# Conditioning vectors in two parts: mixing shift and scale first in row slabs on four column groups, the rest in the natural projection

## What is computed

```python
def adaln(c, w_ada, b_ada):
    return jnp.split(jax.nn.silu(c) @ w_ada + b_ada, 6, axis=-1)   # c: one row each for prompt and sample

def modulate(x, g, shift, scale):
    return rmsnorm(x, g) * (1.0 + scale[:, None, :]) + shift[:, None, :]

p_sh1, p_sc1, p_gt1, p_sh2, p_sc2, p_gt2 = adaln(c_prompt, w_ada[l], b_ada[l])
s_sh1, s_sc1, s_gt1, s_sh2, s_sc2, s_gt2 = adaln(c_sample, w_ada[l], b_ada[l])
...
qa, ka, va, qb, kb, vb, qi, ki, wi = jnp.split(h @ w_in, offs, axis=-1)      # h = modulate(x, g_mix_pre, sh1, sc1)
...
bias = rel_table[:, clip(rel, -128, 128) + 128]                              # by relative position, both attentions
...
yp = yp + p_gt1[:, None, :] * rmsnorm(mp, g_mix_post[l])
```

## Time and profile before

| | us |
|---|---|
| median of three runs | 1901.26 |
| the three runs | 1900.42, 1901.26, 1905.14 |
| the profiled execution | 1904.8 |
| its span, first instruction to last | 1902.9 |

### The profile page before, as it was taken

One profiled execution on the slowest core, in us unless ns is written; L12 is line 12 of the kernel. 1 busy time (PEld: TensorE's weight loads), 2 busy tenths in 40 slices (PEclk: granted clock), 3 DMA queues, 4 the chain that ended last, 5 costly groups with the idle time before them and its releaser, 6 DMA issues. The chain is left out here.

```text
span 1902.9 us, 23599 instructions
## 1 busy us (share of the span) xinstructions
PE 1767.8 (93%) x9129; PEld 1384.4 (73%) x9129; DVE 818.4 (43%) x1600; ACT 657.1 (35%) x1213; POOL 162.6 (9%) x282
## 2 busy tenths in 40 slices
PE   7889799999879988899999579999999999999997
PEld 1145399995357865566665279999999999787876
DVE  0031156667899986555443141111111111455454
ACT  1010144545599963333332151111111111344333
POOL 1100000004311101211110100000000000102020
PEclk9999999999989988899999779999999999999999
DMA  9954431103000012100000221111111111643442
GB/s 339 285 108 50 121 110 45 45 23 134 1 1 1 1 45 92 45 23 23 23 23 15 106 77 44 44 46 53 44 44 44 44 44 44 233 147 125 145 144 100
DMA packets 105534, 146.61 MB, mean 77 GB/s; under 512 B 12346, under 2 KB 71810, under 8 KB 105414
## 3 DMA queue, kind: packets, MB, share of 16 engines
q1 hardware_dynamic: 103468, 139.95, 24.0%
q0 software_dynamic: 1984, 5.57, 1.0%
HBM read 128.51 MB, written 18.96 MB: 77 GB/s over the span
## 5 line engine op out<-in xcount | busy, mean ns | idle before, releaser
L1374 PE MATMUL ps<-h_hi,w_hi 128*128 128x352 f32 x1056 | 341.6, 323 | 8.1 <-DVE w_lo L1414 8.1
L1374 PE MATMUL ps<-h_lo,w_hi 128*128 128x352 f32 x1056 | 339.2, 321 | 0.0
L1374 PE MATMUL ps<-h_hi,w_lo 128*128 128x352 f32 x1056 | 338.9, 321 | 0.0
L920 PE MATMUL ps<-arena 128*128 128x512 f32 (+5 forms) x464 | 181.6, 508 | 32.7 <-DVE small L1112 17.2
L1374 PEld LDWEIGHTS ps<-h_hi,w_hi 128*128 128x128 f32 x1056 | 198.8, 188 | 8.2 <-DVE w_lo L1414 8.2
L1374 PEld LDWEIGHTS ps<-h_lo,w_hi 128*128 128x128 f32 x1056 | 199.1, 189 | 0.0
L1374 PEld LDWEIGHTS ps<-h_hi,w_lo 128*128 128x128 f32 x1056 | 198.5, 188 | 0.0
L907 PE MATMUL ps<-arena 128*128 128x64 f32 (+2 forms) x1280 | 165.7, 267 | 8.1 <-DVE arena L978 3.2
L907 PEld LDWEIGHTS ps<-arena 128*128 128x128 f32 (+2 forms) x1280 | 154.5, 186 | 12.3 <-ACT arena L978 3.6
L1414 DVE TENSOR_TENSOR w_lo<-raw_weights,w_hi 128x1024 fp32r<-128x1024 f32 x44 | 53.7, 1222 | 233.4 <-ACT w_hi L1388 233.4
L920 PEld LDWEIGHTS ps<-arena 128*128 128x128 f32 (+1 forms) x464 | 78.2, 194 | 96.8 <-issue 64.3
(11 more groups left out here) (182 smaller groups left out, 2544.4 us busy)
## 6 DMA issues: line engine op xcount, KB each, us to landing
raw_weights<-in_w_down SPq DMA_DIRECT2D x66, 512.0 KB, 3.3
arena<-in_w_ada SPq DMA_DIRECT2D x12, 2048.0 KB, 14.5
raw_weights<-in_w_gate SPq DMA_DIRECT2D x22, 512.0 KB, 3.7
raw_weights<-in_w_up SPq DMA_DIRECT2D x22, 512.0 KB, 3.7
arena<-in_w_in SPq DMA_DIRECT2D x16, 512.0 KB, 3.7
arena<-in_x_prompt SPq DMA_DIRECT2D x4, 1024.0 KB, 16.9
arena<-in_w_out SPq DMA_DIRECT2D x2, 2048.0 KB, 10.5
arena<-in_x_prompt SPq DMA_DIRECT2D x8, 512.0 KB, 3.5
```

Source lines behind the costliest of these rows:

```text
L920: mm = nc.tensor.matmul(ps_cols(B, s_col(s) + lo, hi - lo, r), q, key_source(t, h, lo, hi), start=True, stop=True)
L1374: mm = nc.tensor.matmul(B(3 * i + c, CH), cut[i][a][:, P * k:P * k + P], h[:, NTOK * k + CH * c:NTOK * k + CH * (c + 1)], start=(k == 0 an ...
```

## The change

`conditioning` and `natural` become one block, `front`.

- `w_ada` is read by rows instead of by columns: 24 slabs (`load_slab`), each with eight-KB pieces for 128 partitions, 2048 columns, and one eighth of the contraction. Slabs 0 to 7 hold shift and scale of the mixing, 8 to 15 those of the FFN, 16 to 23 both gates. They go through six slots of 1 MB.
- For each slab TensorE makes four products of 512 columns. The results lie on partitions 0, 32, 64 and 96 of one bank (`B(bank, 512, 2, 32 * j)`), so on four column groups of the array, and build up over eight slabs.
- Slabs 0 to 7 are loaded first, with x between them. Their four rows are copied out by ACT and DVE, turned by 16 small transposes on TensorE (`L447`), and DVE adds biases that POOL has loaded as columns. The way through the DRAM scratch is gone for these.
- Slabs 8 to 23 are loaded behind the projection's weights, and TensorE takes two of them behind each tile of the natural projection from the second tile on. DVE adds the biases for four rows behind tile 5 and for four behind the last tile. The FFN's shift and scale still go through the scratch, on POOL's queue.
- The two strip writes move from SP, ahead of the turn, to POOL, behind a wait for all 24 slabs. SP's wait for them stays at the end of the block.

The diff, cut to its core:

```diff
-            conditioning(**S)
-            natural(**S)
+            front(**S)
...
-            for c in range(12):
-                if c >= 3:
-                    sp.wait_ge(ada_mm, c - 2)
-                sp.dma_start(T3(QA + 4096 * (c % 3), KT, 512), w_ada[:, :, 512 * order[c]:512 * order[c] + 512]).then_inc(ada_in[c % 3], 16)
...
+    def load_slab(sp, i):
+
+        m, t = i // KT, i % KT
+        if i >= 6:
+            sp.wait_ge(slab_mm, i - 5)
+        if m < 2:
+            sp.dma_start(T(slab_at(i), 2048), w_ada[:, t, 3 * D * m:3 * D * m + 2 * D]).then_inc(slab_in[i % 6], 16)
+        else:
+            sp.dma_start(T3(slab_at(i), 2, D), w_gates[:, t, :, 2 * D:3 * D]).then_inc(slab_in[i % 6], 16)
...
         @block.sync
         def _(sp):
-
-            sp.dma_start(d_strip_a, view(T(STRIPS, 1, HEADS), [[0, P], [1, STRIP_A]])).then_inc(strip_out, 16)
-            sp.dma_start(d_strip_b, view(T(STRIPS + STRIP_A, 1, HEADS), [[0, P], [1, STRIP_B]])).then_inc(strip_out, 16)
...
+            for i in range(KT):
+                load_slab(sp, i)
+                if 1 <= i < 5:
+                    sp.dma_start(T3(x_at[2 * i - 2], 2, D), xp[:, 2 * i - 2:2 * i, :]).then_inc(x_in[i - 1], 16)
...
+            for i in range(KT, NSLAB):
+                load_slab(sp, i)
             sp.wait_ge(nat_mm, NT)
             for n in range(3):
                 load_wb(n, sp, ins, T3).then_inc(wb_in[n], 16)
+            sp.wait_ge(row_dve, 10)
+            for j in range(4):
+                at = row_columns(2, j)
+                sp.dma_start(d_ada[:, at:at + 512], T(ADA_ROWS + 512, 512, 2, 32 * j)).then_inc(gates_out, 16)
...
             sp.wait_ge(strip_out, 32)
+            sp.wait_ge(gates_out, 64)
             ctx.nat_stored = stored
...
+            for m in (1, 2):
+                for j in range(4):
+                    at = row_columns(m, j)
+                    pool.dma_start(T(ADA_BIAS + 512 * (m - 1), 512, 2, 32 * j), ins["b_ada"][0, at:at + 512].partition_broadcast(2)).then_inc(brow_in, 16)
+            pool.wait_ge(row_dve, 6)
...
+            pool.wait_ge(strip_done, 3)
+            pool.wait_ge(slab_mm, NSLAB)
+            pool.dma_start(d_strip_a, view(T(STRIPS, 1, HEADS), [[0, P], [1, STRIP_A]])).then_inc(strip_out, 16)
+            pool.dma_start(d_strip_b, view(T(STRIPS + STRIP_A, 1, HEADS), [[0, P], [1, STRIP_B]])).then_inc(strip_out, 16)
...
+            def slab(i):
+                pe.wait_ge(slab_in[i % 6], 16 * (i // 6 + 1))
+                m, k = i // KT, i % KT
+                bank = (6, 4, 5)[m]
+                for j in range(4):
+                    mm = nc.tensor.matmul(B(bank, 512, 2, 32 * j), sc[:, k, :], T(slab_at(i) + 512 * j, 512),
+                                          start=(k == 0), stop=(k == KT - 1))
+                mm.then_inc(slab_mm, 1)
...
+            for j in range(4):
+                pe.wait_ge(*((row_act, j + 1) if j < 2 else (row_dve, j - 1)))
+                for i in range(4):
+                    mm = nc.tensor.transpose(B(0, 2, c0=2 * (4 * j + i)), T(twice + 512 * j + P * i, P, 2), ident[0:2, 0:2])
...
                 mm.then_inc(nat_mm, 1)
+                if t:
+                    slab(KT + 2 * t - 2)
+                    slab(KT + 2 * t - 1)
             pe.wait_ge(doubled, 2 * NT)
+            pe.wait_ge(row_dve, 10)
...
+                if t in (5, SAMPLE):
+                    m = 1 if t == 5 else 2
+                    dve.wait_ge(brow_in, 128)
+                    dve.wait_ge(slab_mm, KT * m + KT)
+                    for j in range(4):
+                        nc.vector.tensor_tensor(T(ADA_ROWS + 512 * (m - 1), 512, 2, 32 * j), B(3 + m, 512, 2, 32 * j),
+                                                T(ADA_BIAS + 512 * (m - 1), 512, 2, 32 * j), ALU.add).then_inc(row_dve, 1)
```

More of the change, by code:

```diff
@@ new lines, in _ @@
+        @block.scalar
+        def _(act):
+            act.wait_ge(c_in, 32)
+            nc.scalar.activation(T3(R_SC, KT, 2), T3(R_C, 2, KT).rearrange("p c t -> p t c"), ACT.Silu).then_inc(silu_done, 1)
+            act.wait_ge(ss_zero, 1)
+            for t in range(NT):
+                r = rows_of(t)
+                act.wait_ge(x_sem(t), 16)
+                if t:
+                    act.wait_ge(ss_done, t)
+                nc.scalar.activation(T(junk, D, r), T(x_at[t], D, r), ACT.Square,
+                                     accum_out=T(R_SS + t, 1, r)).then_inc(ss_done, 1)
+            act.wait_ge(slab_mm, KT)
+            for j in range(2):
+                nc.scalar.copy(T(twice + 512 * j, 512, 2), B(6, 512, 2, 32 * j)).then_inc(row_act, 1)
+            act.wait_ge(mod_done, 4)
+            turn_read(nc, act, 0, turned, ht_act, ht_at, 0, T, B)
+            for t in range(NT):
+                r = rows_of(t)
+                act.wait_ge(nat_mm, t + 1)
+                nc.scalar.copy(T(NAT + NAT_W * t + 512, NAT_W - 512, r), B(1 if t % 2 else 7, NAT_W - 512, r)).then_inc(nat_act, 1)
+            k_read(act, 0, k_act)
@@ new lines, in _ @@
+            for i in range(KT):
+                if i == 2:
+                    pe.wait_ge(tab_in, 48)
+                    nc.tensor.matmul(B(7, STRIP_B, HEADS), T(tab_b, HEADS, BUCKETS), T(hot_b, STRIP_B, BUCKETS),
+                                     start=True, stop=True).then_inc(strip_mm, 1)
+                slab(i)
+            pe.wait_ge(ident_done, 3)
+            for j in range(4):
+                pe.wait_ge(*((row_act, j + 1) if j < 2 else (row_dve, j - 1)))
+                for i in range(4):
+                    mm = nc.tensor.transpose(B(0, 2, c0=2 * (4 * j + i)), T(twice + 512 * j + P * i, P, 2), ident[0:2, 0:2])
@@ L469, in _ @@
                 mm.then_inc(k_turned, 1)
[L471 to L481 removed]
+        @block.vector
@@ new lines, in _ @@
+            dve.wait_ge(col_mm, 1)
+            dve.wait_ge(cols_in, 64)
+            for j in range(2):
+                got = view(B(0, 1, c0=16 * j), [[1, 2], [2, KT]])
+                bias = view(T(R_BCOL + 8 * j, 1), [[0, 2], [1, KT]])
+                nc.vector.tensor_tensor(T3(R_MOD + 16 * j, 2, KT), got, bias, ALU.add).then_inc(col_done, 1)
+            dve.wait_ge(col_done, 2)
+            for c in range(2):
+                nc.vector.scalar_tensor_tensor(T(R_SCALE + 8 * c, KT), T(R_MOD + 16 + 8 * c, KT), 1.0,
+                                               T(R_G, KT), ALU.add, ALU.mult).then_inc(mod_done, 2)
@@ L490, in _ @@
+            dve.wait_ge(mod_done, 4)
             turn_read(nc, dve, 1, turned, ht_dve, ht_at, 0, T, B)
@@ L506, in _ @@
             k_read(dve, 1, k_dve)
+            dve.wait_ge(mod_in, 64)
+            for c in range(2):
+                nc.vector.scalar_tensor_tensor(T(R_SCALE + 16 + 8 * c, KT), T(R_MOD + 48 + 8 * c, KT), 1.0,
+                                               T(R_G + 8, KT), ALU.add, ALU.mult).then_inc(mod_done, 2)
 NCH = 3
```

235 lines of the change are left out of this document (93 added, 142 removed).

## The result

| | before | after |
|---|---|---|
| median | 1900.84 us (4 runs, 1900.26 to 1905.14) | 1949.27 us (4 runs, 1945.37 to 1957.82) |
| the profiled execution | 1904.8 | 1946.45 |
| its span | 1902.9 | 1944.7 |

The ratio is 1.0256, with a 95% interval from 1.0216 to 1.0296. The changed kernel is 48 us slower by the medians and 41.8 us by the spans of the profiled executions. The difference of 6 us between these two is scatter: the runs of the changed kernel lie 12 us apart and the profiled one is among its fastest, while that of the kernel before was above its median.

A forecast was written before the change was run, and what follows sets the result against it. TensorE bounds the first block, and a block ends with its last engine, SP's waits included. Projection start 57 + 101.9 + 27, strips 100, barrier 0.5: 286.5 against 236.2, +50 us; forecast 1952 us, range 1934 to 1985.

The forecast's parts named there:

- projection starts: Natural projection's first matmul: at about 57 us instead of 120, 63 us gained.
- projection with slabs: TensorE in the projection: 101.9 us as before plus 27 us for sixteen slabs, ending at 186 us.
- from the slabs' end to the block's end: Strips bare behind the last slab: 100 us including 3 for stores beside them, plus 0.5 us barrier.
- block's end: Mark where the next block is released: 286.5 us against 236.2 before, so +50 us.
- First phase: Block's start: 8th slab in at 37 to 39 us, DVE's scalings end last at about 42, projection starts 63 us earlier.
- The slabs: Sixteen slabs on TensorE in the projection: four steps of 0.427 us each, partial overlap of column groups, S = 27 us.
- rival B: Full overlap of the column groups: S = 14 to 16 us, mark +37 us, 1938 us; chance 0.15.
- rival A: No overlap of the column groups: S = 54.6 us, mark +78 us, 1979 us; chance 0.34.
- The rate of the strips: Strip writes on POOL's queue: about 50 GB/s from eight partitions, share near 0.46, 96.8 us as before.
- rival C: Strips fast on POOL's queue: 12 us, hidden by the stores; 1866 us with S = 27; chance 0.11 (faster).
- The stores: SP's stores at the block's end run beside the strips and add 3 us to them.

The follow-up runs named there:

- experiment 9: Changed kernel with the 64 products of slabs 8 to 23 all on the first column group, in four banks; 1994.23 us, ratio 1.0484.
- experiment 1: Kernel before with only the two strip writes moved to POOL's queue, behind the natural projection's last tile; 1992.52 us, ratio 1.0473.
- experiment 4: Changed kernel with the strips issued early on SyncE's queue, behind the projection's weights and ahead of slabs 8 to 23; 1923.61 us, ratio 1.0110.
- experiment 5: Changed kernel with the strips last on SyncE's own queue, behind its stores, instead of on POOL's; 1954.69 us, ratio 1.0271.
- experiment 2: Changed kernel with POOL's wait ahead of the strips at 18 slabs instead of 24; 1926.68 us, ratio 1.0132.
- experiment 6: Changed kernel with the same strip writes at the same place and queue, read from 128 partitions instead of 8; 1866.29 us, ratio 0.9820.
- experiment 8: Changed kernel with strips written 16 times instead of 128, behind slab 18, and read back in 16 loads of 16 partitions; 1873.52 us, ratio 0.9846.

## Why the prediction was right, and where it was not

The sign and the mechanism held: the strips lie bare at the block's end, the barrier releases the next block behind them, and the kernel is slower. The sum, step by step, in us of the profiled execution:

| step | predicted | measured |
|---|---|---|
| projection starts | 57 | 56.6 |
| projection with slabs | 101.9 + 27 | 101.9 + 15.6 = 117.5 |
| from the slabs' end to the block's end | 100.5 | 103.7 |
| block's end | 286.5 | 277.8 |

The medians stand closer (1952 and 1949.27) than the sum deserves: it put the profiled execution at 1954.8 and this was 1946.45. Some 6 of these 8.4 us were given back by scatter: I took the median to lie 3.5 us under the profiled execution, and it lay 2.8 above.

*First phase.* Right, in its chain as well. One reading was wrong: the loads moved 325 GB/s from 10 to 20 us and 396 only from 20 on the earlier trace rows, not 395 from 12.5 us; the sum allowed for it (8th slab at 37 to 39), and TensorE took that slab at 38.32. DVE's scalings end last, at 42.42 against a predicted 42:

```profile
30.58 1.06 ACT L410 ACTIVATE arena<-arena 128x1024 f32<-128x1024 f32 x1 [3.28 <-DMA arena<-in_x_prompt]
...
36.38 6.04 DVE L497 TENSOR_SCALAR arena<-arena,small 128x1024 f32<-128x1024 f32 x9 [1.96 <-POOL small L380]
```

*The slabs.* This is the term that failed: predicted 27 us, measured 15.6. The step was "the second must follow the first, and only the second of one group can run beside the first of the next". The first half is true, experiment 9 shows it at 0.43 us a step. The second is not: it wants 3.4 us for a pair of slabs on two groups and on four alike. Two groups took 3.53, four took 1.83. It is rival B's size, which I had held down with the two instructions of a product; they are in order within a group and hold up no other. Serial products (rival A, at 0.34 nearly as likely as the forecast) are what experiment 9 shows, 1994 us with its copies and one wait of 3.85 us. The Trainium skill (TensorE: Matmul & The Clock Gate, Packing small matmuls) gives 2.38 times for three groups; for fp32 products of 512 columns the runs show 1.97 times for two and 3.8 for four (6.95 against 3.53 and 1.83 us); three were not run.

*The rate of the strips.* Right in what mattered, 50 to 53 GB/s on either queue (experiments 1, 4, 5), and rival C, the fast queue, is out: 0.11 of the chances lay there. But its argument foresaw a share near 0.46, and the first strip took 0.97. Rival C had reasoned that more engines might mean more speed; they came, and moved the same.

*The stores.* The predicted 100.5 us is 96.8 for the strips, 3 for the stores and 0.5 for the barrier. The stage took 103.7: 97.8 from the slabs' end to the strips' landing and 5.9 from there to the release. That is near, but the mechanism was another: I took the stores as traffic that slows the strips. The second strip landed 96.0 us after its issue, as ever. It was the stores that stood behind the strips, issued until 277.13, 5 us beyond the strips' landing. That the size came out within some 3 us was luck; experiment 2 shows what it costs to think of it that way (13.7 us). The Trainium skill (DMA: Bandwidth & Descriptors, Issuing engines are not separate DMA queues) says that DMAs of all engines share the same 16 and interleave. They do interleave in the trace, but in 190 to 240 us SyncE's queue got 1.2% of the engines' time.

Not tried: moving SyncE's wait for the strips into a later block, so that the next block covers them. The strips' columns are overwritten there by its own buffers, so the wait could not go without a new place for the source.

## What to carry to other kernels

Before a DMA is moved to where nothing covers it, divide its bytes by the rate that its own rows show, and ask how many partitions it reads: a source of eight partitions moved about 50 GB/s on each queue and at each place, and held up what was issued beside it (from GpSimd's queue) or behind it (on SyncE's). Spreading the source over all partitions (a small write to DRAM and a read back) was worth more than any place tried: 1949 to 1866 us, and 1858 once the transfer also had a cover. In this kernel, with its barrier at each block's end, a wait there belongs to the path of every engine, even if the data is needed much later.

## What the runs showed of the hardware

- A DMA from eight partitions on GpSimd's queue occupied 16 engines (0.97) and on SyncE's 7.5 (0.47), at 53 and 50 GB/s. In the first case a 512 KB store on SyncE's queue landed 45 us after its issue (12 us in experiment 6, 7 in the kernel before).
- The second strip, with rows of 1536 bytes, took 0.475 of the engines on the same GpSimd queue. Why the first took twice that is open.
- Loads from DRAM into 16 partitions at a time moved 112 GB/s at a share of 1.1 (experiment 8); two loads into 128 partitions with the same bytes went at 234 to 292 GB/s in windows of experiment 6.
- Four, two and one column groups gave 0.92, 1.77 and 3.48 us for a slab of four fp32 products of 512 columns.
- In the first 40 us, before the turn, a slab of eight instructions took 1.89 us, as long as a pair of slabs in the projection (1.90), though the granted clock in those windows reads 1.00, that is 2.4 GHz. TensorE had stood idle for 0.6 to 6.9 us ahead of each of them. The kernel before shows the same at its start: the first instructions of TensorE's products, from 12.48 us on, stand 0.85 us apart, and 0.43 later. It hardly mattered here, since the slabs' loads set the pace; its cause stays open.

```profile
10.00:20.00 10.00, 5.22 (x18) 0.31 (x18) 1.16 (x3) 2.42 (x5) 0.00 (x0) 1.00 1.01 369
```

```profile
27.42 1.89 PE L433 MATMUL ps<-arena,small 128*2 128x512 f32 x8 [3.15 <-DMA arena<-in_w_ada]
```
